# 32-row expert blocks on four column tiles, a ring of ten weight units, and attention scores over 64 partitions

## The reference, cut to what matters

```python
s = jnp.einsum('bqgnd,bkgd->bgnqk', qb, kw) * scale     # heads of 64 channels
p = masked_softmax(s, mask_w)
```

```python
def expert_block(args):
    xb, e = args
    hg, hu = jnp.split(xb @ w_gu[e], 2, axis=-1)      # w_gu[e]: 1024 x 1024
    return (jax.nn.silu(hg) * hu) @ w_down[e]         # w_down[e]: 512 x 1024
```

## Time and profile before

| | us |
|---|---|
| median of 3 runs | 3789.73 (3787.17 to 3801.17) |
| the profiled execution's own time | 3786.93 |
| its span | 3785.1 |
| PE busy | 3227.8 (85%) |
| DVE busy | 1270.8 (34%) |
| ACT busy | 1002.7 (26%) |
| POOL busy | 399.6 (11%) |

### The profile page before, as it was taken

How to read it: one execution, slowest core, us unless ns; L and a number is a source line. 1 busy time by engine, 2 the same in 40 slices (tenths; PEclk the granted TensorE clock), 3 DMA queues, 4 the chain that set the end, 5 groups by cost and what they waited for, 6 DMA issues and landing times. The chain is left out here.

```text
span 3785.1 us, 47531 instructions
## 1 busy us (share of the span) xinstructions
PE 3227.8 (85%) x18903; PEld 2025.2 (54%) x18903; DVE 1270.8 (34%) x1922; ACT 1002.7 (26%) x1668; POOL 399.6 (11%) x543
## 2 busy tenths in 40 slices
PE   7987989999896999989787877896897986878985
PEld 5765667878664688777452222232466863322332
DVE  3343434332546433222731100012595553100112
ACT  2333422221334221122621111111342332111212
POOL 1012310000302000000000000001121230000002
PEclk9989999999998999999888988998898998989997
DMA  7335323332411332322058999973113126999996
GB/s 194 82 113 205 140 52 93 100 94 61 107 34 53 84 94 82 107 78 82 31 207 327 390 391 395 393 288 92 39 50 78 39 57 257 388 394 390 385 388 242
DMA packets 442385, 669.66 MB, mean 177 GB/s; under 512 B 86709, under 2 KB 310882, under 8 KB 440938
## 3 DMA queue, kind: packets, MB, share of 16 engines
q1 hardware_dynamic: 416121, 601.45, 45.8%
q0 software_dynamic: 11936, 34.85, 3.1%
q10 hardware_dynamic: 14160, 30.94, 2.2%
HBM read 632.03 MB, written 35.13 MB: 176 GB/s over the span
## 5 line engine op out<-in xcount | busy, mean ns | idle before, releaser
L1834 PE MATMUL moe_ps<-moe_wgu,moe_xbT 128*64 128x512 f32 x2496 | 601.1, 638 | 120.1 <-DMA moe_wdn<-in_moe_w_down 119.0
L1834 PEld LDWEIGHTS moe_ps<-moe_wgu,moe_xbT 128*64 128x64 f32 x2496 | 189.5, 147 | 523.4 <-issue 522.0
L1845 PE MATMUL moe_ps<-moe_wdn,moe_hT 128*64 128x512 f32 x1248 | 285.0, 598 | 36.9 <-ACT moe_hT L1901 36.9
L181 PE MATMUL ffn_in_ps<-ffn_xhi,ffn_in_whi 128*128 128x512 f32 x704 | 280.6, 399 | 14.0 <-DVE ffn_xlo L323 14.0
L182 PE MATMUL ffn_in_ps<-ffn_xlo,ffn_in_whi 128*128 128x512 f32 x704 | 280.2, 398 | 0.0
L183 PE MATMUL ffn_in_ps<-ffn_xhi,ffn_in_wlo 128*128 128x512 f32 x704 | 280.0, 398 | 0.0
L2008 DVE TENSOR_TENSOR moe_gated_h<-moe_gated_h,moe_ps 128x256 f32<-128x256 f32 x78 | 32.8, 421 | 686.2 <-ACT moe_gated_h L1898 686.2
L1898 ACT ACT_TABLE_LOAD x78 | 100.1, 1283 | 475.3 <-issue 475.3
L1845 PEld LDWEIGHTS moe_ps<-moe_wdn,moe_hT 128*64 128x64 f32 x1248 | 82.7, 136 | 189.1 <-issue 133.6
L2012 DVE COPY moe_y<-moe_ps 128x512 f32<-128x512 f32 x78 | 54.0, 692 | 345.2 <-PE moe_ps L1845 345.2
L181 PEld LDWEIGHTS ffn_in_ps<-ffn_xhi,ffn_in_whi 128*128 128x128 f32 x704 | 133.4, 190 | 48.0 <-issue 15.6
(11 more groups left out here) (675 smaller groups left out, 5948.5 us busy)
## 6 DMA issues: line engine op xcount, KB each, us to landing
moe_wgu<-in_moe_w_gu SPq DMA_DIRECT2D x64, 4096.0 KB, 31.6
moe_wdn<-in_moe_w_down SPq DMA_DIRECT2D x64, 2048.0 KB, 31.5
ffn_came<-in_ffn_w_in SPq DMA_DIRECT2D x88, 512.0 KB, 5.0
na_modw<-in_ada_w SPq DMA_DIRECT2D x10, 4096.0 KB, 12.5
expert_rows<-moe_y ACTq DMA_DIRECT2D x156, 128.0 KB, 6.1
da_in_w<-in_attn_w_qkv SPq DMA_DIRECT2D x12, 1024.0 KB, 5.2
ro_w<-in_rw_w_rkv SPq DMA_DIRECT2D x24, 512.0 KB, 4.0
ffn_came<-in_ffn_w_out SPq DMA_DIRECT2D x8, 1408.0 KB, 7.3
```

Source lines behind the costliest of these rows:

```text
L181: nc.tensor.matmul(ps[0:width, slot * tiles + o], whi[:, slot, k, cols], xhi[:, k], start=(k == 0), stop=False)
L1834: last = nc.tensor.matmul(psGU[q * BLK:(q + 1) * BLK], xbT[:, k], cols[:, q], start=(k == 0), stop=(k == KD - 1))
L1845: last = nc.tensor.matmul(psY[q * BLK:(q + 1) * BLK], hT[:, k % 2, (k // 2) * BLK:(k // 2 + 1) * BLK], wdn[:, s, k, q * 512:(q + 1) * 512] ...
```

## The change

`BLK` becomes 32. A block's 32 rows take 32 columns of the array, and each k-step is four matmuls in the array's four column tiles: gate and up are computed in two halves (`a` = 0, 1) of 8 k-steps with four matmuls of 128 columns, down in 4 k-steps with four of 256. Each quarter row of a token is gathered as its own 1 KB row, so that `xg` holds 128 partitions of 256 columns, and DVE's 32x32 transpose turns it into `xbT` in one instruction; `h` is turned by DVE likewise. PE has no transposes left in the loop. ACT copies `y` (two buffers) and issues four stores of 32 rows of 1 KB. POOL, ACT and DVE run the blocks in pairs (`each_pair`), two buffers each, so that a layer with an odd number of blocks gets one block more without products. POOL gathers two blocks ahead.

The weights lie in `ring`: ten units of 2 MB (16 KB in a partition), three for an expert. A unit is loaded when the one ten before it is free.

```diff
-BLK = 64
+BLK = 32
 MAXB = EXPERTS + 2 * SEQ // BLK
-SLOTS = 3
+ROOM = MAXB + 4
+UNITS = 10
+PARTS = 3
...
-            wgu = sb(s2, "wgu", [P, SLOTS, KD, 2 * HID])
-            wdn = sb(s2, "wdn", [P, SLOTS, KH, D])
-            xrow = wdn[:, SLOTS - 1]
+            ring = sb(s2, "ring", [P, UNITS, KH, D])
+            xrow = ring[:, UNITS - 1]
...
+            def each_pair(eng, body):
+                pairs = (block_count(eng) + 1) >> 1
+                body(0, 0, 0)
+                body(1, 1, 0)
+                with eng.Fori(1, pairs) as j:
+                    body(j * 2, 0, j)
+                    body(j * 2 + 1, 1, j)
+                return pairs
...
+                for u in range(UNITS - 1):
+                    load(u)
+                sp.wait_ge(x_stored, 16 * TC)
+                load(UNITS - 1)
                 sp.wait_ge(plan_ready, 1)
-                for e in range(SLOTS, EXPERTS):
-                    end = end_of(sp, e - SLOTS)
-                    sp.wait_ge(gu_done, end)
-                    load_gu(e)
-                    sp.wait_ge(down_done, end)
-                    load_down(e)
+                for u in range(UNITS, PARTS * EXPERTS):
+                    e, part = (u - UNITS) // PARTS, (u - UNITS) % PARTS
+                    if part != 1:
+                        end = end_of(sp, e)
+                        sp.wait_ge(down_done if part == 2 else gu_done[1], end)
+                    load(u)
...
+                def gather(b, s, j, spare=None):
+                    if not (isinstance(b, int) and b < 2):
+                        pool.wait_ge(gathered[s], j * 16)
+                        pool.wait_ge(x_ready, b)
+                        pool.sem_inc(pick_begun, 1)
...
-                def expert_block(b, s):
-                    pe.wait_ge(b_taken, (b + 1) * 2)
-                    for k in range(KD):
-                        cols = wgu[:, s, k].rearrange("p (g q n) -> p q g n", g=2, q=2)
-                        for q in range(2):
-                            last = nc.tensor.matmul(psGU[q * BLK:(q + 1) * BLK], xbT[:, k], cols[:, q], start=(k == 0), stop=(k == KD - 1))
-                    last.then_inc(gu_done, 1)
-                    turn_x(b + 1)
-                    pe.wait_ge(h_ready, b + 1)
-                    for m in range(2):
-                        last = nc.tensor.transpose(psH[:, m * P:(m + 1) * P], h[:, m * P:(m + 1) * P], B.ident[:])
-                    last.then_inc(h_turned, 1)
-                    pe.wait_ge(h_taken, b + 1)
+                def expert_block(b, e):
+                    pe.wait_ge(x_ready, b + 2)
+                    for a in range(2):
+                        for k in range(KD):
+                            cols = ring[:, (PARTS * e + k // KH) % UNITS, k % KH].rearrange("p (g a m j i) -> p a j g m i", g=2, a=2, m=2, j=4)[:, a]
+                            for j in range(4):
+                                last = nc.tensor.matmul(psGU[j * BLK:(j + 1) * BLK, a], xbT[:, k], cols[:, j], start=(k == 0), stop=(k == KD - 1))
+                        last.then_inc(gu_done[a], 1)
                     pe.wait_ge(y_taken, b + 1)
                     for k in range(KH):
-                        for q in range(2):
-                            last = nc.tensor.matmul(psY[q * BLK:(q + 1) * BLK], hT[:, k % 2, (k // 2) * BLK:(k // 2 + 1) * BLK],
-                                                    wdn[:, s, k, q * 512:(q + 1) * 512], start=(k == 0), stop=(k == KH - 1))
+                        if k % 2 == 0:
+                            pe.wait_ge(h_ready, b * 2 + k // 2 + 1)
+                        for j in range(4):
+                            last = nc.tensor.matmul(psY[j * BLK:(j + 1) * BLK], hT[:, k * BLK:(k + 1) * BLK], ring[:, (PARTS * e + 2) % UNITS, k, j * 256:(j + 1) * 256],
+                                                    start=(k == 0), stop=(k == KH - 1))
                     last.then_inc(down_done, 1)
...
+                def turn_x(s, j):
+                    dve.wait_ge(gathered[s], j * 16 + 16)
+                    V.transpose(scratch[:, 0:KD * BLK], xg[:, s]).then_inc(x_ready, 1)
+
+                def gate_and_turn(b, s, j):
+                    for a in range(2):
+                        dve.wait_ge(silu_done, b * 2 + a + 1)
+                        V.tensor_tensor(h[:, a], gated[:, a], psGU[:, a, HD:P], ALU.mult).then_inc(h_made, 1)
+                        dve.wait_ge(h_made, b * 2 + a + 1)
+                        V.transpose(hT[:, a * HD:(a + 1) * HD], h[:, a]).then_inc(h_ready, 1)
+                    turn_x(1 - s, j + s)
...
                 for h in range(2):
-                    nc.tensor.matmul(psS[:, v % 2, h, 0:n], projT[:, it, i * P:(i + 1) * P], kz[:, b, it // 4, h, 0:n], start=True, stop=False)
+                    half = slice(h * HD, (h + 1) * HD)
+                    nc.tensor.matmul(psS[:, v % 2, h, 0:n], projT[half, it, i * P:(i + 1) * P], kz[half, b, it // 4, 0:n], start=True, stop=False)
+                for h in range(2):
                     last = nc.tensor.matmul(psS[:, v % 2, h, i * P:n], B.ident_b[:], B.causal_b[:], start=False, stop=True)
...
-                    for h in range(2):
-                        half = slice(h * HD, (h + 1) * HD)
-                        last = nc.vector.scalar_tensor_tensor(out=kz[half, b, a, h], in0=projT[half, t], scalar=B.cols("k_gain", 1 + b, 1)[half],
-                                                              in1=psD[half, u % 4], op0=ALU.mult, op1=ALU.mult)
-                    last.then_inc(scaled, 1)
+                    nc.vector.scalar_tensor_tensor(out=kz[:, b, a], in0=projT[:, t], scalar=B.cols("k_gain", 1 + b, 1), in1=psD[:, u % 4],
+                                                   op0=ALU.mult, op1=ALU.mult).then_inc(scaled, 1)
```

208 lines of the change are left out of this document (92 added, 116 removed).

## The result

The changed kernel takes 3634.31 us, the median of 4 runs (3630.3 to 3637.28); the kernel before took 3795.45 beside it (4 runs, 3787.17 to 3802.72). The ratio is 0.9575, with a 95% interval from 0.9549 to 0.9601.

What follows compares the result with a forecast made beforehand. Weights bound layer 1 and layer 0 up to expert 26, then PE; in the attention, a loop over DVE and POOL. Terms -61 - 32 + 5 - 11 = -99 took 3786.9 to 3688, forecast 3690 us, range 3655 to 3745.

Steps and rivals of the forecast that it cites:

- the DMA engines' time: Both mixtures: weights take about 510 us of a layer; each block adds its gathers and stores, 1.65 us before, 0.85 after.
- Own traffic of a block: Gathers and stores in the mixtures: 0.85 us a block for 1.65, layer 1 19 us less; upper bound 2.2 us, +50.
- the rival in which the DMA engines gain nothing: Mixtures: 1 KB rows cost 1.65 us per 32-row block, so the kernel takes 3740 us or so; chance 0.12.
- The block of 6.0 us: Layer 0 from expert 26: 3.8 gate-up, 1.8 down, 0.1 and 0.3 waits; 21 blocks, 32 us less.
- two tiles abreast: Mixtures: gate-up runs two column tiles at once, 54 ns an instruction, block 9.1 us, kernel 3769 us; chance 0.07.
- the block of 10.9 us: Mixtures: both products two abreast, or small matmuls bound by issue and weight load; kernel slower, 3881 us; chance 0.09.
- The clock in the mixtures: Nearly every expert begins at 1.2 GHz, its block some 9 us, hidden behind weights but for 3 us at a burst's start.
- The gap at the start: Start of each mixture: one more unit under way and an earlier, shorter first gate-up cut time without transfers by 9 us.
- The ends: Ends of the mixtures: four stores for two, and layer 1's 52nd block without products (+3); +5 us in all.
- The attention: NSA attention: faster scores over 64 partitions, limited by a loop over DVE and POOL; 9 us less, between 0 and 27.
- The rival by which the stage gives nearly all of its 30 us: NSA attention: faster scores save nearly 30 us, 16 more than forecast, kernel 3674 us; chance 0.12.
- `kz`: Stage before the attention: DVE's 8 instructions become four of the same length; 2 us less.

Runs made afterwards that it cites:

- nine_gather_32: The changed kernel with nine ring units in place of ten and a block's 32 rows gathered as 32 pieces of 4 KB into 32 partitions; ratio 0.9664.

## Why the prediction was right in direction and short by 50 us

- **The step that failed: the DMA engines' time.** What was missing is a term of the sum, put at nothing without a reason: what the change does to the rate of the weights' own queue. The record took the rate of the weights' queue as given ("The weights take 27.8% x ... put simply, 108.15 MB in 92.7% of 300 us, so 201.3 MB take about 510 us of a layer") and charged a block only with its own packets, 1.65 us. But that rate was itself depressed, by two things that the change removes. One is the place of the slots: 11 and 17 us in the two layers. The other is the slowing of the weights beside a gather of 64 rows of 4 KB into 64 partitions. Of the gather's 17.7 and 23.6 us, its own packets are 1.4% of 300 us for 18 or 19 blocks, some 0.27 us a block, 7 and 10, which the record has in its 1.65; the neighbours' 10 and 13 it hasn't. Together 21 and 30 us are outside the sum, nearly all that the two layers gave beyond the forecast there (20 and 35). The place of the slots was luck: nothing in the change aims at it.
- **Own traffic of a block**: 0.85 us forecast, 0.74 measured, so 25 us less in layer 1 and not 19. Right in mechanism; its upper bound of 2.2 us was far off, and with it the rival in which the DMA engines gain nothing.
- **The block of 6.0 us**: 5.46 measured. 27.3 ns for an instruction of gate-up where 30 were taken (within its 27 to 54), 61 ns of down where 57 were; 0.8 us at an expert's bound, spread over its blocks less than the 0.3 taken. The burst gave 36.9 for 32. The rivals of two tiles abreast and of the block of 10.9 us are out.
- **The clock in the mixtures**: PE does begin nearly every expert at the low level, and it is hidden, as written: 6.06 us of gate-up at 2392.58 behind a wait of 9.06 for weights. The cold block took 7.8 us, not 9.
- **The gap at the start**: in layer 1 the windows lack (59 x 0.09 + 46 x 0.01) / 1.03 = 5.6 us, where they lacked 14.6: 9.0, with 9 forecast. In layer 0, from the first load to expert 26, the packets' times lack 16.8 us of a share of 1.03 before and 7.5 after, so 9.3; 4.3 of them are the tenth unit's.
- **The ends**: +5 forecast, +2.8 measured behind the last product of layer 1, where ACT has the 52nd block's copies and four stores still to do (1.75 us for four stores). That is the record's +3 for this block.
- **The attention**: -9 forecast, 0 measured. The unchanged step of 3.58 us was right. What the record gave to the other steps, a faster PE, didn't come: PE's clock fell with its work, in a stage in which it waits. The record reckoned with the clock in the mixtures and left it out here. With the clock of before, the estimate from the eight profiles is 283 us against 293.6, so the term itself seems right and the missing one is the clock. The rival by which the stage gives nearly all of its 30 us is out: the shortest of the eight profiles is 6 us below before.
- **`kz`**: -2 forecast, -2.4 measured.

Measured pieces for layer 0 to expert 26: place 11, neighbours 10, own traffic 27 x 1.65 - 29 x 0.74 = 23, gap 9. They make 53 where 49.5 were measured; the 3.5 are not explained. For layer 1 to its end: place 17, neighbours 13, own traffic 25, gap 9, which is 64 where 67.3 were measured; the record's 4 for the shorter block behind the last weights would fill it, but no run shows that piece by itself.

## What to carry to other kernels

Where transfers are the bound, work out the time of one packet before pricing a change: bytes of the main queue over its own share of time, in stretches with and without other traffic. If the same 4 KB take 159 ns in one place and 164 or 233 in another, look for the start of the tile (here a multiple of 256 bytes) and for small transfers into part of the partitions. In this kernel these two edits alone give 1.6% of the 4.2%, without another loop.

Of a stage in which PE waits for others, price the clock with the products: less work there may lower the granted clock (here from 31 us at the lower level to 61), and the stage then keeps its length. And compare more than one profile: the same attention code took 287.6 to 298.1 us in eight of them.

## What the runs showed of the hardware that was not expected

- A 4 KB packet into slots 64, 128 or 448 bytes past a multiple of 512 took 2 to 3% longer than at 0 or 256 past (162.7 and 162.9 against 159.5 ns in the changed kernel, 168.3 against 164.0 in the one before).
- A gather of 64 rows of 4 KB into 64 partitions slowed not only its own packets (233 ns for 159 to 168) but also the weights' beside them (208 ns on average), for 1.6 to 3.3 us.
- In the attention with the narrow scores, each us at the lower of PE's two clock levels went with 0.32 us more of the stage, over eight profiles.
- Four tiles of 32 columns with 128 moving columns ran at 27.3 ns an instruction, weight load included.
- The same loop of 160 instructions of products ran at 5.46 us a block in one program and at 6.0 in another, with a hole of 0.19 us without a releaser, in nearly all blocks of an expert but its first. Nine units are not the cause, since nine_gather_32 has them at 5.46. The cause is open.
